# Eight projection slabs as seven-product block pairs, with the sums on GpSimd

## What is computed

```python
h = rmsnorm(x, norm_mix_g[layer])
proj = h @ w_in[layer]
q_a, k_a, v_a, q_b, k_b, v_b, gl_a, gl_b = jnp.split(proj, SPLITS, axis=-1)
```

## Time and profile before

| | |
|---|---|
| median of 3 runs | 1399.18 us (1398.53 to 1399.27) |
| the profiled execution | 1398.27 us |
| its span in the trace | 1396.5 us |
| TensorE busy | 1388.6 us (99%) |
| VectorE, ScalarE, GpSimd busy | 922.0, 594.8, 212.2 us |
| granted TensorE clock | 1.00 over the span |

### The profile page before, as it was taken

One profiled execution on the slowest core, in us unless ns is written; L12 is line 12 of the kernel. 1 busy time (PEld: TensorE's weight loads), 2 busy tenths in 40 slices (PEclk: granted clock), 3 DMA queues, 4 the chain that ended last, 5 costly groups with the idle time before them and its releaser, 6 DMA issues.

```text
span 1396.5 us, 21351 instructions
## 1 busy us (share of the span) xinstructions
PE 1388.6 (99%) x8522; PEld 1173.8 (84%) x8522; DVE 922.0 (66%) x1256; ACT 594.8 (43%) x842; POOL 212.2 (15%) x214
## 2 busy tenths in 40 slices
PE   9999999999999999999999999999999999999998
PEld 7887888777888989989888997778888998989886
DVE  6635432766767759587656678656756957758775
ACT  4324531554444445353244345344434535344353
POOL 5000000000022302112333020000022221302310
PEclk9999999999999999999999999999999999999999
DMA  5224123211336846635332222232235764927573
GB/s 185 91 91 114 61 65 109 69 56 41 115 106 151 209 108 159 167 96 149 103 102 83 91 69 76 81 100 78 90 96 148 176 160 112 213 90 196 135 178 109
DMA packets 152811, 161.58 MB, mean 116 GB/s; under 512 B 4010, under 2 KB 140564, under 8 KB 152740
## 3 DMA queue, kind: packets, MB, share of 16 engines
q1 hardware_dynamic: 120820, 129.12, 29.0%
q0 software_dynamic: 31904, 31.46, 12.5%
q10 hardware_dynamic: 16, 0.00, 0.0%
HBM read 157.68 MB, written 2.10 MB: 114 GB/s over the span
## 4 chain that ended last, share of the span: by engine, by line
PE 99%; DVE 1%; ACT 0%; issue 0%; POOL 0%; DVEq 0%; POOLq 0%; ACTq 0%
PE ps L2376 63%; PE ps L2441 17%; PE ps L2372 4%; PE ps L2398 4%; PE ps L2514 3%; PE ps L2584 1%; PE ps L2765 1%; PE ps L2792 1%; PE ps L2778 1%; PE ps L2883 1%; PE ps L2671 0%; PE ps L2962 0%; PE ps L2561 0%; PE ps L2714 0%; PE ps L2732 0%; PE ps L2678 0%
## 5 line engine op out<-in xcount | busy, mean ns | idle before, releaser
L2376 PE MATMUL ps<-AA,wh 128*128 128x512 f32 x1440 | 453.9, 397 | 0.0
L2376 PE MATMUL ps<-BB,wh 128*128 128x512 f32 x1088 | 342.2, 396 | 0.6 <-DVE wl L1469 0.4
L2376 PEld LDWEIGHTS ps<-AA,wh 128*128 128x128 f32 x1440 | 267.5, 188 | 69.7 <-issue 6.9
L2376 PE MATMUL ps<-AA,wl 128*128 128x512 f32 x720 | 283.3, 394 | 0.0
L935 ACT ACTIVATE wh<-raw 128x1024 fp32r<-128x1024 f32 (+2 forms) x149 | 141.5, 950 | 259.6 <-PE ps L2376 205.4
L2376 PEld LDWEIGHTS ps<-BB,wh 128*128 128x128 f32 x1088 | 202.1, 188 | 50.5 <-issue 2.1
L1469 DVE TENSOR_TENSOR wl<-raw,wh 128x1024 fp32r<-128x1024 f32 (+2 forms) x149 | 170.4, 1143 | 74.3 <-ACT wh L935 74.0
L2376 PE MATMUL ps<-BB,wl 128*128 128x512 f32 x544 | 213.9, 393 | 0.0
L2376 PEld LDWEIGHTS ps<-AA,wl 128*128 128x128 f32 x720 | 135.5, 188 | 30.9
L2376 PEld LDWEIGHTS ps<-BB,wl 128*128 128x128 f32 x544 | 102.3, 188 | 23.2
L2441 PE MATMUL ps<-Hl,wh 128*128 128x256 f32 x384 | 107.6, 280 | 0.0
(11 more groups left out here) (404 smaller groups left out, 2353.6 us busy)
## 6 DMA issues: line engine op xcount, KB each, us to landing
raw<-in_w_in SPq DMA_DIRECT2D x38, 1024.0 KB, 5.5
raw<-in_w_ff SPq DMA_DIRECT2D x31, 1024.0 KB, 5.4
raw<-in_w_mlp_in SPq DMA_DIRECT2D x16, 1024.0 KB, 5.5
raw<-in_w_mlp_out SPq DMA_DIRECT2D x16, 1024.0 KB, 5.0
zf<-in_w_mlp_out POOLq DMA_DIRECT2D x48, 256.0 KB, 4.7
zf<-in_w_ff POOLq DMA_DIRECT2D x48, 256.0 KB, 4.7
raw<-in_w_out SPq DMA_DIRECT2D x8, 1024.0 KB, 5.0
arena<-in_x SPq DMA_DIRECT2D x4, 512.0 KB, 7.7
```

The lines of the kernel that those rows point to most:

```text
L2376: last = pe.matmul(dense_psum(t_ps, kind), a[:, k, :], b[:, o0 + k, col0:col0 + S1], start=start, stop=stop)
```

## The change

Slabs 4 to 11 are made in four **pairs** q = 0 to 3. A pair's weights are seen as four blocks (inner half by slab) and the tokens as four (inner half by token half, 256 tokens). Instead of 48 matmuls of 128x512, a pair takes seven products of 12 matmuls of 128x256, whose operands are blocks or sums of blocks, and whose results are put together from four PSUM banks:

- **Token sums, once**: GpSimd multiplies the gain onto the two upper token blocks (`XG11`, `XG12`), ScalarE onto the two lower ones (`XG22`, `XG21`), and GpSimd makes `T1`, `T3`, `T2`, `T4`, each 128x1024. Each is split (ScalarE high, VectorE low) into `TX`.
- **Weight sums, each pair**: GpSimd makes S3 and S1 (into `F`), then S2 and S4 (into `SQ`), each 128x512. They are split too (`Qh`, `Ql`, and slot 0 of `wh`, `wl`), as are the unsummed block A11 (`upper_left`) and A12, A22 (`lower`).
- **Results**: ScalarE copies two banks (`qk_mid`), VectorE adds the two others to it, and TensorE may go on only then: product 5 waits for the copy (`q_mid`), product 7 for the addition. VectorE then writes one quarter of the pair's output from PSUM and `qk_mix`, and GpSimd multiplies the three other quarters by `RS` (`pair_out`).
- **Moved**: GpSimd's iotas come after its sums of pair 1, its masks after all pairs; the distance biases of VectorE into pair 1; the class copies two per pair; the transposes of `RS` for the value slabs behind the last pair. The iota's integers and the biases' scratch lie in memory of `BB` (`spare`).

The diff, cut to its core (`after` makes GpSimd wait for its own instruction):

```diff
+        T_PAIRS, PAIRS = T_QKV_A + 4, 4
+        later = range(1, PAIRS)
+        SUMS = ["T1", ("S3", 0), ("S1", 0), ("S2", 0), "T3", "T2", ("S4", 0), "T4"]
+        for i in later:
+            SUMS += [(s, i) for s in ("S3", "S1", "S2", "S4")] + [(c, i - 1) for c in ("C22", "C21", "C12")]
+        SUMS += [(c, PAIRS - 1) for c in ("C22", "C21", "C12")]
+        HIGHS = ["X22", ("S13", 0), ("A11", 0), "T1", ("S2", 0), "X21", "T3", "T2", ("S4", 0), "T4"]
+        LOWS = [("S13", 0), ("A11", 0), "T1", ("S2", 0), "T3", "T2", ("S4", 0), "T4"]
+        for i in later:
+            HIGHS += [("A11", i), ("S13", i), ("S24", i)]
...
             convert_first(3, hi_ready)
             pool.memset(epsb[:, :], EPS).then_inc(consts_ready, 1)
             pool.wait_ge(consts_ready, 2)
+            def gained(dst, half):
+                g = vecT[:, G_MIX:G_MIX + 4].unsqueeze(2).to_broadcast([P, 4, HB])
+                after(pool.tensor_tensor(dst, X[:, 0:4, META + half * HB:META + (half + 1) * HB], g, ALU.mult))
+            def third_and_first(q):
+                p = pair_load(q)
+                pool.wait_ge(w_landed[p % 2], 16 * (p // 2 + 1))
+                if q > 0:
+                    pool.wait_ge(parts_lo, low(("S13", q - 1)))
+                pool.tensor_tensor(blk(F[:, 0, 0:S1]), quarter(p, 0, 0), quarter(p, 1, 0), ALU.subtract)\
+                    .then_inc(sums_done, 1)
+                pool.tensor_tensor(blk(F[:, 1, 0:S1]), quarter(p, 1, 0), quarter(p, 1, 1), ALU.add)\
+                    .then_inc(sums_done, 1)
...
+                pool.tensor_tensor(blk(SQ[:, 1, 0:S1]), blk(F[:, 1, 0:S1]), quarter(pair_load(q), 0, 0), ALU.subtract)\
+                    .then_inc(sums_done, 1)
...
+                pool.tensor_tensor(blk(SQ[:, 0, 0:S1]), quarter(pair_load(q), 0, 1), blk(SQ[:, 1, 0:S1]), ALU.subtract)\
+                    .then_inc(sums_done, 1)
...
+            def pair_out(q):
+                i = 2 * q + 4
+                r = [RS[:, h * HB:(h + 1) * HB] for h in range(2)]
+                pool.wait_ge(q_mid, 3 * q + 3)
+                pool.wait_ge(evac_done, T_PAIRS + 2 * q + 2)
+                for slab_no, half, src in ((i + 1, 1, qk_mid[:, 1]), (i + 1, 0, qk_mix[:, 0]), (i, 1, qk_mix[:, 1])):
+                    pool.tensor_tensor(qk_half(slab_no, half), token_half(slab_no, src), token_half(slab_no, r[half]),
+                                       ALU.mult).then_inc(sums_done, 1)
+
+            pool.wait_ge(gain_ready, 1)
+            pool.wait_ge(xt_copied, 2)
+            pool.wait_ge(xt_copied_act, 2)
+            gained(XG11, 0)
+            gained(XG12, 1)
+            pool.tensor_tensor(T1_SUM, XG12, XG11, ALU.subtract).then_inc(sums_done, 1)
+            third_and_first(0)
+            second(0)
+            pool.wait_ge(parts_hi, high("X22"))
+            pool.tensor_tensor(T3_SUM, XG22, XG12, ALU.subtract).then_inc(sums_done, 1)
+            pool.wait_ge(sums_done, summed("T3"))
+            pool.tensor_tensor(T2_SUM, XG22, T1_SUM, ALU.subtract).then_inc(sums_done, 1)
+            fourth(0)
+            pool.wait_ge(sums_done, summed("T2"))
+            pool.wait_ge(parts_hi, high("X21"))
+            pool.tensor_tensor(T4_SUM, XG21, T2_SUM, ALU.subtract).then_inc(sums_done, 1)
+            pair_sums(1)
             for c in range(4):
                 rows = slice(32 * c, 32 * c + 32)
                 pool.iota(DI0[rows, :], pattern=[[-1, 256]], base=P + c, channel_multiplier=4).then_inc(di_ready, 1)
                 pool.wait_ge(di_ready, 2 * c + 1)
                 pool.iota(DI4[rows, :], pattern=[[-1, 128]], base=96, channel_multiplier=1).then_inc(di_ready, 1)
                 pool.wait_ge(di_ready, 2 * c + 2)
+            pair_out(0)
+            for q in range(2, PAIRS):
+                pair_sums(q)
+                pair_out(q - 1)
+            pair_out(PAIRS - 1)
+            pool.wait_ge(sums_done, summed(("C12", PAIRS - 1)))
...
+            gained(XG22, 1)
+            first_sums(0)
+            upper_left(0)
+            token_high(1, T1_SUM)
+            act.wait_ge(slab_done, 3)
+            second_sum()
+            act.wait_ge(sums_done, summed("T1"))
+            gained(XG21, 0)
+            token_high(3, T3_SUM)
+            token_high(2, T2_SUM)
+            fourth_sum()
+            lower(0)
+            act.wait_ge(parts_lo, low("T1"))
+            token_high(4, T4_SUM)
+            act.wait_ge(x_diag, 5)
+            for q in range(PAIRS):
+                done, base = 6 * q, 4 * (q % 2)
+                if q + 1 < PAIRS:
+                    act.wait_ge(q_blk, done + 1)
+                    upper_left(q + 1)
+                act.wait_ge(q_blk, done + 2)
+                if q > 0:
+                    act.wait_ge(sums_done, summed(("C12", q - 1)))
+                act.activation(qk_mid, ps[:, base + 2:base + 4, 0:HB], ACT.Copy).then_inc(q_mid, 1)
+                to_classes(2 * q)
+                to_classes(2 * q + 1)
+                if q + 1 < PAIRS:
+                    act.wait_ge(q_blk, done + 4)
+                    first_sums(q + 1)
+                    act.wait_ge(q_blk, done + 5)
+                    last_sums(q + 1)
+                    lower(q + 1)
+                else:
+                    convert(T_V_A)
...
+            def first_sums(q):
+                dve.wait_ge(parts_hi, high(("S13", q)))
+                dve.tensor_tensor(Ql[:, 1:3], F[:, :, 0:S1], Qh[:, 1:3], ALU.subtract).then_inc(parts_lo, 1)
+            def token_low(i, src):
+                dve.wait_ge(parts_hi, high(f"T{i}"))
+                dve.tensor_tensor(t_part(i, 1), src, t_part(i, 0), ALU.subtract).then_inc(parts_lo, 1)
...
+            first_sums(0)
             dve.wait_ge(stat_done, 1)
             dve.tensor_copy(RS[:, 0:S1], ps[:, 7, :]).then_inc(x_diag, 1)
...
-            for t in range(T_QKV_A + 3, T_GATE_A + 1):
-                if t - 1 < T_V_A:
-                    dve.wait_ge(slab_done, t)
-                    dst, src = qkv_a(t - 1, dense_psum(t - 1, ONE))
-                    dve.tensor_tensor(dst, src, qkv_a(t - 1, RS[:, 0:S1])[1], ALU.mult).then_inc(evac_done, 1)
-                elif t in (T_VW_A, T_GATE_A):
+            upper_left(0)
+            plain(2)
+            token_low(1, T1_SUM)
+            second_sum()
+            token_low(3, T3_SUM)
+            token_low(2, T2_SUM)
+            plain(3)
+            fourth_sum()
+            late_scale(0)
+            lower(0)
+            token_low(4, T4_SUM)
+            late_scale(1)
+            vectors()
+            for q in range(PAIRS):
+                i, base, last = 2 * q + 4, 4 * (q % 2), q + 1 == PAIRS
+                if not last:
+                    upper_left(q + 1)
+                if q == 1:
+                    distances()
+                to_classes(2 * q)
+                to_classes(2 * q + 1)
+                dve.wait_ge(q_blk, 6 * q + 4)
+                dve.wait_ge(q_mid, 3 * q + 1)
+                dve.tensor_tensor(qk_mid, qk_mid, ps[:, base:base + 2, 0:HB], ALU.add).then_inc(q_mid, 1)
+                if last:
+                    convert(T_V_A)
+                else:
+                    first_sums(q + 1)
+                    last_sums(q + 1)
+                dve.wait_ge(q_blk, 6 * q + 6)
+                dve.tensor_tensor(qk_half(i, 0), token_half(i, ps[:, base + 2, 0:HB]), token_half(i, RS[:, 0:HB]), ALU.mult)
+                dve.wait_ge(slab_done, T_PAIRS + 2 * q + 2)
+                dve.wait_ge(q_mid, 3 * q + 2)
+                if q > 0:
+                    dve.wait_ge(sums_done, summed(("C12", q - 1)))
+                dve.tensor_tensor(qk_mix, ps[:, base + 1:base + 4:2, 0:HB],
+                                  qk_mid[:, 0:1].to_broadcast([P, 2, HB]), ALU.add).then_inc(evac_done, 2)
+                dve.tensor_tensor(qk_mid[:, 1], qk_mid[:, 0], qk_mid[:, 1], ALU.add).then_inc(q_mid, 1)
+                if not last:
+                    lower(q + 1)
+
...
-            for t in range(2, T_GATE_A):
...
-                elif t < T_V_A:
-                    full_slab(t, Ah, Al, 0, ONE)
...
+            def qk_product(a, b, bank, first):
+                for k in range(4):
+                    for i, (w, x) in enumerate(((a[0], b[0]), (a[0], b[1]), (a[1], b[0]))):
+                        mm = pe.matmul(ps[:, bank, 0:HB], w[:, k, :], x[:, k, :], start=(first and k == 0 and i == 0),
+                                       stop=(k == 3 and i == 2), skip_group_check=True)
+                return mm
...
+            for q in range(PAIRS):
+                g1, g2, g3, g4 = pair_banks(q)
+                if q == 1:
+                    pe.wait_ge(x_diag, 5)
+                    pe.wait_ge(vec_ready, 1)
+                    pe.wait_ge(meta_copied, 1)
+                if q >= 2:
+                    pe.wait_ge(evac_done, T_PAIRS + 2 * q - 2)
+                pe.wait_ge(parts_lo, low(("A11", q)))
+                qk_product(A11_, B11_, g1, True).then_inc(q_blk, 1)
```

(51 more changed lines are left out.)

171 lines of the change are left out of this document (138 added, 33 removed).

## The result

The changed kernel takes **1421.15 us** (median of 4 runs, 1420.42 to 1421.91), the kernel before 1398.86 us beside it (1397.93 to 1399.27). The ratio is 1.0161, with a 95% interval of 1.0148 to 1.0173: 22.3 us slower, where the prediction had 1410 with 1401 to 1417.

What follows compares the result with a forecast made beforehand. TensorE was taken as the bound. Terms 2.5 + 4.7 + 7.1 + 3.9 - 4.9 gave +13.3 us, the other order +9.7; the middle, +11.5, on 1398.27 gave 1410, range 1401 to 1417.

Steps and rivals of the forecast that it cites:

- the rule on two-input instructions: VectorE instructions with two SBUF inputs and GpSimd additions never run together; the later waits for the whole of the earlier.
- step 5: Pairs 1 to 3: product 5 waits for ScalarE's copy, 1.0 us a pair, plus distance biases in pair 1; +3.9 or +4.7.
- both sums: Whole change, by which engine wins when both stand ready: +13.3 us with engines alternating, +9.7 in the other order.
- The products: Slabs 4 to 11: four seven-product pairs take 39.7 us where eight slabs took 44.6; 4.9 us off TensorE's stream.
- Steps 1 and 2: Slabs 0 to 2: VectorE's low parts wait for GpSimd's gain products and T1; slab 2 starts at 23.95, +2.5 us.
- Step 3: Before pair 0: four small diagonal low parts wait for GpSimd sums, delaying stats(0) and pair 0; +4.7 us or 0.
- in turns: Case where VectorE and GpSimd alternate, so each small diagonal low part waits for a whole GpSimd sum; total +13.3 us.
- the two orders: Engines alternating, or VectorE's queued instructions going one after another; no row decides, so the middle, +11.5 us, was taken.
- Step 4: Pair 0: waits of 0.5, 1.5, 0.5 and 4.7 us ahead of products 2, 3, 6 and 7; +7.1, other order +7.4.
- the clock too: Rival: granted clock falls to its lower level behind two waits near 4.7 us; +3 to +8, 1413 to 1418; chance 0.12.
- The rival on the other side: No hold-up between VectorE and GpSimd: waits of 1.8 and 1.1 us ahead of product 7, pairs 0 and 1; 1396.2; chance 0.09.

Runs made afterwards that it cites:

- e10: Changed kernel with GpSimd writing each block once with a constant instead of its sums and multiplications, values left out: 1397.46 us, ratio 0.9990.
- e2: Changed kernel with GpSimd's T3 beginning only when the small diagonals are written: 1420.54 us, ratio 1.0160.
- e3: Changed kernel with distances and iotas moved after the pairs' sums, their scratch in F and SQ: 1418.0 us, ratio 1.0145.
- e7: Kernel before, with two gain products and four 128x1024 sums added on GpSimd whose results nobody reads: 1407.1 us, ratio 1.0061.
- e4: Changed kernel with extra TensorE matmuls into unused banks ahead of the four long waits: 1419.53 us, ratio 1.0154.
- e6: Changed kernel with GpSimd's sums and output multiplications on VectorE and distance biases moved into the value slabs: 1407.82 us, ratio 1.0066.

## Why the prediction was wrong, and where it was right

Right were the direction, the rule on two-input instructions, and the places of the waits up to pair 0 (but for product 2, which had none). Of the later ones only that ahead of product 5 of pair 3 stood where it was expected. The sum was short by 10.8 us. The step that failed is step 5, and beside it the clock, which both sums put at nothing. Step by step:

- **The products.** -4.9 predicted, -4.2 measured (44.6 against the 40.4 of e10).
- **Steps 1 and 2**, +2.5: over-sized. Slab 2 starts at 21.96, 0.5 later than before. VectorE's low part that stood at 15.48 started at 14.67, as the weights had landed earlier in this execution, and lasted 1.89, until 0.5 us after the first gain product. The gain products take 2.1 us each (4.20 for two from 14.11) where 2.4 was taken. T1 (18.39 to 20.81) was all but over when the low part of slab 2 had its high part (20.53), and held it up by 0.1 (1.37 us). In e2, e3 and e7, where GpSimd began its gain products 0.8 to 1.0 us later, slab 2 starts at 22.8 to 22.9.
- **Step 3**, +4.7 "in turns" or 0: the engines take turns, and the wait is 4.72. That the size fits is luck. The step had all four small instructions wait, until 35.7; two of them were held up, by T3 and T2, and `stats(0)` came at 33.90. TensorE was ready for it at 29.2 and not at 30.9. That pair 0 starts at 41.23, where 41.1 was worked out, is chance too: the lower clock put 2.0 us back on. e7 shows the step by itself. The "middle" of the two orders, which I took for the forecast, is what no row supports.
- **Step 4**, pair 0, +7.1: 0.68 + 0.31 + 4.00 = 5.0 measured, the large one ahead of product 7 as said.
- **Step 5 is the one that failed**: pairs 1 to 3, +3.9 as worked out, 9.3 measured (5.36, 1.18, 2.71). It had a wait of 1.0 ahead of product 5 of each pair, for ScalarE's copy behind GpSimd's multiplications, and 0.7 to 1.2 more for the distance biases. Pairs 1 and 2 have no such wait; in pair 3 it is 2.71. The largest, 5.36, stands ahead of product 7 of pair 1, where the step had none, for VectorE's addition. The step held up only VectorE's low parts. But the distances took 8.3 us (62.63 to 70.90) where they took 3.6 before, beside GpSimd's last multiplication and four sums, and the two class copies of the next pair up to 2.97. Sums of 128x512, taken as 1.0 us, last 1.30 to 1.34 alone. e3 takes the distances away and pair 1's wait goes with them, though only 3.1 us of time. The section of the Trainium skill that the prediction cites (SBUF — State Buffer, "Who interferes with whom") names copies and multiplications by a number as well.
- **The rival "the clock too"**, 0.12: it occurred, behind four waits where two were thought of, also behind one of 2.71 us. At its full price, 6.6 us, it lies in the +3 to +8 given, but the forecast's sums have it at nothing. What it is worth is less where VectorE is the bound: e4 takes 4.9 us of it away and gives back 1.6.
- **The forecast's last step**: the two orders were averaged (+11.5) where the turns gave +13.3. Put right are turns (+1.8), step 5 (+5.4), products (+0.7), and less in steps 1, 2 and 4 (-4.1); that makes 1414. With the clock by e4's third of its price (+2.2) one comes to 1416, with its full price (+6.6) to 1420. The measured 1421 is nearer the second. The terms don't simply add up: VectorE is the bound from 24 to 84 us, and what one wait loses another, or the clock, takes over (e2, e3, e4). How the last 5 us are shared between clock and hold-ups stays open.

The rival on the other side, 1396.2, was right about how the form runs with nearly free sums (e10, 1397.5) and wrong about what the sums cost on GpSimd. Two of the recorded sums are off by 0.1: step 4's four waits make 7.2, and this rival's 1396.3.

**Could it be made to pay?** Not by what was tried: with sums that cost next to nothing the form gains 1.3 us (e10), and with real ones, in the best placement tried, it loses 9.5 us (e6). Sums on ScalarE were not tried. Nor were pairs for the later slabs alone, where VectorE would have the slabs' own room for the token sums; e10's saving of TensorE time, about 1 us a pair, bounds what those could give.
